# Halved up products, stores and splits on GpSimd, and all ending gathers at once, in a two-layer transformer and mixture-of-experts kernel

## The chip, the cores and the metric

The kernel runs on one core of one Trainium2 chip. The time is the device time of that core in microseconds (us). Before the change it is 2076.37 us, the median of three runs (2075.52 to 2078.95). The engines are TensorE (PE in the profile; PEld is its loading of weights), VectorE (DVE), ScalarE (ACT), GpSimd (POOL) and SyncE (SP). SyncE, ScalarE and GpSimd can issue DMAs.

## The reference

512 tokens of width 1024 go through two transformer layers, then through a third layer whose feed-forward part is a mixture of 16 experts. Only this last part and the ending are touched:

```python
def hier_moe(h, lp):                      # h: 512 tokens x 1024
    g_logits = h @ w_router_group + b_router_group            # 4 groups
    p_group = softmax(g_logits); g_sel = argmax(g_logits)
    e_sel = logits of the 4 experts of that group
    top_v, top_i = top_k(e_sel, 2)
    w_top = softmax(top_v) * p_group[g_sel]
    for e in range(16):
        a = silu(h @ w_gate[e]) * (h @ w_up[e])               # 1024 x 512 each
        y = y + combine[e] * (a @ w_down[e])                  # 512 x 1024
x = x + gate2 * rmsnorm(y, g_post_ffn)
```

All values are float32. Each product is made of three float32r products of a high and a low part of both operands (high x high, low x high, high x low).

## The kernel before

**Routing.** TensorE computes the logits of the router and transposes the normalised tokens; VectorE and ScalarE copy them, and they are stored as `h2_tokens` in HBM. A chain of some 60 small VectorE operations (`seq`), with two exponentials on ScalarE and a few small matmuls, gives each pair of token and expert a slot in a list in which every expert's slots start at a multiple of 128. `seq` waits each time for all that VectorE, ScalarE and TensorE have been given so far. GpSimd scatters the token numbers into the list `slot_token`.

**The expert loop.** A block is 128 slots of one expert. There are 18 blocks in this run; the last one stands behind the loop. A block's weights are 12 units of 128 x 1024: units 0 to 3 are the gate weights, 4 to 7 up, 8 to 11 down. In a block:
- SyncE reads the next block's expert number and fetches that block's 12 units into a ring of 12 buffers (`fetch`, L2201). Each fetch waits until the unit of this block that lies in the buffer has been split.
- ScalarE copies a unit's high part (`split_unit`, L2209), and VectorE subtracts it from the unit, which gives the low part (L2211). Six split units can be held, and they are made four ahead of the products (`split_ahead`).
- TensorE makes 24 gate matmuls and 24 up matmuls (`wide`), each with 512 columns, then waits for the product of silu(gate) and up (`av`, VectorE, L2275), transposes it (4 transposes, L2280), transposes the next block's gathered tokens (8 transposes, `turn_rows`, L2178), waits for the split of the transposed hidden values (ScalarE L2285, VectorE L2287), and makes 24 down matmuls.
- GpSimd gathers the token rows of a later block (`gather`, L2170: 128 rows of 4 KB by an indirect DMA). It does nothing else in the loop. The statement stands in the middle of the block, but GpSimd waits only until the rows gathered last have been transposed, so it runs ahead of the others: as soon as TensorE has transposed the rows for block b + 1, in the middle of block b, the gather for block b + 2 is issued.
- ScalarE and VectorE copy the two halves of the output (L2307, L2310), and SyncE stores it to `slot_output` in HBM (L2313). SyncE waits for the copies first, so it fetches nothing meanwhile.

All queues run in the order in which the code is written; what one engine needs from another it waits for on a semaphore (`reach`).

**The ending.** For each of four groups of 128 tokens GpSimd gathers the two output rows of each token (L2348), two groups at most in flight. VectorE and ScalarE weight and add them, normalise them and add the tokens, which TensorE transposes; ScalarE stores the result.

## Time and profile before

| | |
|---|---|
| Median of three runs | 2076.37 us |
| The profiled execution | 2073.45 us |
| Its span, first to last instruction | 2072.0 us |
| Mean granted TensorE clock | 0.927 |
| TensorE busy | 1820.4 us (88%) |
| VectorE, ScalarE, GpSimd busy | 1227.8, 874.9, 109.5 us |
| Gathers of the expert loop, in number | 18 |
| Stores of a block's output, in number | 18 |

The times in the rows below are microseconds from the start of the span; a matmul's row begins where it begins and has the engine's modelled end, so that the distance between the starts of two matmuls is the pace. "[1.05 <-PE bank L202]" behind a row is the engine's idle time before it and what ended it. A DMA's row is the issuing instruction; when the data has landed is told apart from it. Lines are those of the kernel before.

### The profile page before, as it was taken

How to read it: one execution, taken by the hardware profiler on the slowest of the kernel's cores; microseconds unless marked ns; L12 is line 12 of the kernel's file. 1: busy time of each engine (PE TensorE's matmuls, PEld its weight loads, DVE VectorE, ACT ScalarE, POOL GpSimd, SP SyncE). 2: the span in 40 equal slices, each digit the busy share in tenths (PEclk: the TensorE clock that was granted, in tenths of full speed). 3: DMA queues.
4: the chain of work that ended last, by engine and by line, in shares of the span. 5: the costliest groups of instructions: out<-in, count | busy, mean ns of one | idle time of the engine just before them, and what ended most of it. 6: DMA issues, size and time to landing. Idle time of an engine off the chain costs nothing.

```text
span 2072.0 us, 24514 instructions
## 1 busy us (share of the span) xinstructions
PE 1820.4 (88%) x8710; PEld 1488.0 (72%) x8710; DVE 1227.8 (59%) x2145; ACT 874.9 (42%) x1382; POOL 109.5 (5%) x132
## 2 busy tenths in 40 slices
PE   8897899999998977899999997999687299999982
PEld 7776788888887656788888886866577277777762
DVE  3555668885226555568665226455733388888874
ACT  3346532233215446332323214335622177777761
POOL 1000000000000000001100001000000201001001
PEclk9899899999998989999999997999885599999996
DMA  4323235454331240246543333202110499999963
GB/s 141 94 69 118 62 102 142 133 148 129 100 100 44 71 183 11 71 113 190 163 134 111 102 93 98 82 1 72 51 41 8 166 343 369 361 361 368 359 249 132
DMA packets 224050, 294.57 MB, mean 142 GB/s; under 512 B 13344, under 2 KB 151560, under 8 KB 223832
## 3 DMA queue, kind: packets, MB, share of 16 engines
q1 hardware_dynamic: 205492, 235.36, 34.8%
q0 software_dynamic: 12080, 41.65, 6.4%
q10 hardware_dynamic: 6388, 16.35, 2.1%
q8 instruction: 58, 0.95, 0.2%
q14 instruction: 32, 0.26, 0.0%
HBM read 271.78 MB, written 21.54 MB: 142 GB/s over the span
## 4 chain that ended last, share of the span: by engine, by line
PE 78%; DVE 10%; ACT 7%; issue 2%; DMA 2%; POOL 0%; DVEq 0%; ACTq 0%; POOLq 0%; SPq 0%
PE bank L200 23%; PE bank L202 22%; PE bank L201 22%; PE bank L69 11%; DVE tmp L69 2%; DVE weights_low L227 1%; DMA out_second<-slot_output,pair_slots 1%; ACT weights_high L221 1%; ACT squares L69 1%; DVE z_and_u L69 1%; DVE hidden_low L2287 1%; DVE expert_hidden L2275 1%; PE bank L2280 1%; ACT hidden_high L2285 1%; PE bank L272 0%
## 5 line engine op out<-in xcount | busy, mean ns | idle before, releaser
L227 DVE TENSOR_TENSOR weights_low<-ring,weights_high 128x1024 fp32r<-128x1024 f32 x202 | 246.7, 1223 | 407.4 <-ACT weights_high L221 407.3
L200 PE MATMUL bank<-XH,weights_high 128*128 128x512 f32 x1120 | 454.0, 405 | 30.0 <-DVE XL L69 20.3
L202 PE MATMUL bank<-XH,weights_low 128*128 128x512 f32 x1120 | 444.0, 396 | 0.0
L201 PE MATMUL bank<-XL,weights_high 128*128 128x512 f32 x1120 | 443.3, 396 | 0.0
L221 ACT CAST weights_high<-ring 128x1024 fp32r<-128x1024 f32 x202 | 211.1, 1047 | 439.3 <-PE bank L202 438.2
L200 PEld LDWEIGHTS bank<-XH,weights_high 128*128 128x128 f32 x1120 | 215.4, 192 | 78.7 <-ACT squares L69 12.3
L202 PEld LDWEIGHTS bank<-XH,weights_low 128*128 128x128 f32 x1120 | 214.7, 192 | 47.1
L201 PEld LDWEIGHTS bank<-XL,weights_high 128*128 128x128 f32 x1120 | 215.3, 192 | 42.8 <-issue 0.5
L2211 DVE TENSOR_TENSOR XL<-ring,XH 128x1024 fp32r<-128x1024 f32 x144 | 169.7, 1220 | 31.0 <-ACT XH L2209 31.0
L2209 ACT CAST XH<-ring 128x1024 fp32r<-128x1024 f32 x144 | 143.5, 1046 | 0.0
L69 DVE SCALAR_TENSOR_TENSOR squares<-ring,c_silu,squares 128x128 f32<-128x128 f32 x384 | 135.2, 352 | 13.6
L200 PE MATMUL bank<-hidden_high,weights_high 128*128 128x512 f32 x352 | 137.1, 390 | 0.0
L202 PE MATMUL bank<-hidden_high,weights_low 128*128 128x512 f32 x352 | 137.0, 389 | 0.0
L201 PE MATMUL bank<-hidden_low,weights_high 128*128 128x512 f32 x352 | 136.9, 389 | 0.0
L2211 DVE TENSOR_TENSOR weights_low<-ring,weights_high 128x1024 fp32r<-128x1024 f32 x72 | 86.1, 1218 | 0.1
L189 POOL DMA_DIRECT2D ring<-in_w_ada x48 | 42.5, 885 | 720.0 <-DVE squares L263 720.0
L202 PEld LDWEIGHTS bank<-hidden_high,weights_low 128*128 128x128 f32 x352 | 66.1, 188 | 13.8
L201 PEld LDWEIGHTS bank<-hidden_low,weights_high 128*128 128x128 f32 x352 | 66.1, 188 | 13.8
L200 PEld LDWEIGHTS bank<-hidden_high,weights_high 128*128 128x128 f32 x352 | 66.1, 188 | 13.4
L1111 ACT ACTIVATE tmp<-tmp 128x512 f32<-128x512 f32 x44 | 27.8, 632 | 110.0 <-DVE tmp L1107 110.0
L2209 ACT CAST weights_high<-ring 128x1024 fp32r<-128x1024 f32 x72 | 73.8, 1050 | 0.0
L200 PE MATMUL bank<-XH,hidden_high 128*128 128x512 f32 x144 | 59.9, 416 | 11.7 <-DVE hidden_low L2287 11.7
(445 smaller groups left out, 2953.6 us busy)
## 6 DMA issues: line engine op xcount, KB each, us to landing
ring<-in_w_ffn_in SPq DMA_DIRECT2D x88, 512.0 KB, 4.7
ring<-in_w_gate SPq DMA_DIRECT2D x72, 512.0 KB, 4.9
ring<-in_w_up SPq DMA_DIRECT2D x72, 512.0 KB, 8.5
ring<-in_w_down SPq DMA_DIRECT2D x72, 512.0 KB, 10.5
ring<-in_w_ada POOLq DMA_DIRECT2D x48, 512.0 KB, 4.7
ring<-in_w_ffn_out SPq DMA_DIRECT2D x44, 512.0 KB, 3.5
ring<-in_w_out SPq DMA_DIRECT2D x24, 512.0 KB, 3.5
slot_output<-expert_out SPq DMA_DIRECT2D x18, 512.0 KB, 3.8
```

The costliest lines, as they stand in the source:

```text
L69: op(*args, **kw).then_inc(self.line.sem, 1)
L189: queue.eng.dma_start(dst, src).then_inc(ln.sem, 16)
L200: PE.matmul(out_ap, w_h, x_h, start=first, stop=False, skip_group_check=True)
L201: PE.matmul(out_ap, w_h, x_l, start=False, stop=False, skip_group_check=True)
L202: return PE.matmul(out_ap, w_l, x_h, start=False, stop=last, skip_group_check=True)
L221: S.copy(wh[:, s, :], ring[s][:, :]).then_inc(high_done.sem, 1)
L227: V.tensor_tensor(wl[:, s, :], ring[s][:, :], wh[:, s, :].bitcast(F32), ALU.subtract).then_inc(split_done.sem, 1)
L1111: S.activation(sg, sg, ACT.Silu).then_inc(silu_done.sem, 1)
L2209: S.copy(high[s], raw[q]).then_inc(l_high.sem, 1)
L2211: V.tensor_tensor(low[s], raw[q], high[s].bitcast(F32), ALU.subtract).then_inc(l_split.sem, 1)
L2275: V.tensor_tensor(av[:, :], sg[:, :], bank[1][:, :], ALU.mult).then_inc(l_av.sem, 1)
L2280: t = PE.transpose(bank[6][:, k * P:(k + 1) * P], av[:, k * P:(k + 1) * P], ident)
```

## The change

1. **Up products in halves.** The up matmuls have 256 columns, one half into bank 1 and one into bank 7; there are 48 instead of 24. In unit 7 the first half is finished before the second. `av`, the transposes and the splits of the hidden values are done by halves too; the next block's 8 transposes stand between the two halves' transposes, and the first two down units need only the first half.
2. **Store on GpSimd.** In every block but the last GpSimd issues the store of the output, waits until it has landed, and then tells ScalarE and VectorE that the buffer is free.
3. **Two splits on GpSimd.** The low parts of units 1 and 11 are made by GpSimd.
4. **The gather** for block b + 1 now stands first in block b. On GpSimd's queue that is behind the wait for the store of block b - 1.
5. **Ending.** All 8 gathers are issued at once into buffers of their own; ScalarE does the first weighting and, with the scale and epsilon in it, the root; GpSimd adds the tokens for groups 0 and 1; the gain row is made ahead of the routing chain and the tokens are transposed behind its second exponential (`token_rows`), and `seq` waits only for what it needs.

```diff
+POOLED = (1, 11)
...
-            return vec.do(op, *args, after=[vec.line.now(), act.line.now(), pe.line.now()], **kw)
+            return vec.do(op, *args, after=[vec.line.now(), *after], **kw)
...
+            for c in range(4):
+                k = 4 * half + c
+                t = pe.do(PE.matmul, bank[b][:, c * P:(c + 1) * P], POST_FFN[:, k:k + 1].broadcast_to([P, P]), ident,
+                          start=True, stop=True)
+            bank_free[b] = [act.do(S.copy, grow[:, half * 512:(half + 1) * 512], bank[b][:, :], after=[t])]
...
+                    for c in range(4):
+                        k = 4 * half + c
+                        t = pe.do(PE.transpose, bank[b][:, c * P:(c + 1) * P], X[:, k, t4 * P:(t4 + 1) * P], ident)
+                    bank_free[b] = [act.do(S.copy, x_tok[:, t4, half * 512:(half + 1) * 512], bank[b][:, :], after=[t])]
...
             S.copy(high[s], raw[q]).then_inc(l_high.sem, 1)
-            reach(V, l_high, g + 1)
-            V.tensor_tensor(low[s], raw[q], high[s].bitcast(F32), ALU.subtract).then_inc(l_split.sem, 1)
+            if q in POOLED:
+                reach(G, l_high, g + 1)
+                G.tensor_tensor(low[s], raw[q], high[s].bitcast(F32), ALU.subtract).then_inc(l_pool.sem, 1)
+            else:
+                reach(V, l_high, g + 1)
+                V.tensor_tensor(low[s], raw[q], high[s].bitcast(F32), ALU.subtract).then_inc(l_split.sem, 1)
...
+            if not last:
+                gather(b + 1)
...
+            wait_split(PE, b, 7)
+            up(7, (0,), 0)
+            up(7, (0,), 1).then_inc(l_up.sem, 1)
+            up(7, (1,), 0)
+            up(7, (1,), 1).then_inc(l_used.sem, 1)
+            hidden(0)
+            hidden(1)
+            hidden_turn(0)
+            if not last:
+                turn_rows(b + 1)
+            hidden_turn(1)
             reach(S, l_used, b * UNITS)
+            hidden_split(0)
+            hidden_split(1)
             split_ahead(7)
-            if not last:
-                gather(b + 1)
-                turn_rows(b + 1)
...
-            SP.dma_start(yd[bass.ds(b * P, P), :], yt[:, :]).then_inc(l_st.sem, 16)
+            store = SP if last else G
+            reach(store, l_y0, b + 1)
+            reach(store, l_y1, b + 1)
+            store.dma_start(yd[bass.ds(b * P, P), :], yt[:, :]).then_inc((l_last if last else l_st).sem, 16)
+            if not last:
+                G.wait_ge(l_st.sem, b * 16 + 16)
+                G.sem_inc(l_free.sem, 1)
...
         for t4 in range(TT):
+            for j, dst in enumerate((first, second)):
+                G.indirect_dma_start(dst[:, t4, :], None, yd,
+                                     bass.IndirectOffsetOnAxis(ap=slots_u[:, j, t4:t4 + 1], axis=0)).then_inc(
+                    l_pair[t4].sem, 16)
```

GpSimd in the expert loop, before: from the read of the first table entry to the end of the loop.

```order
L2319 TENSOR_LOAD block_expert
L2321 UNCONDITIONAL_BRANCH
L2321 COMPARE_AND_BRANCH
L2166 REGISTER_ALU
L2167 ISA [waits rows_turned]
L2167 COPY tokens_now<-slot_tokens 128x1
L2168 REGISTER_ALU
L2170 DMA gathered<-h_tokens,tokens_now 128x1024 [waits index_set]
L2321 UNCONDITIONAL_BRANCH
```

GpSimd in the expert loop, after (`XL<-ring,XH` is the split of unit 11, `weights_low<-ring,weights_high` that of unit 1 of the next block, `slot_output<-expert_out` the store).

```order
L2191 ISA [waits rows_turned]
L2191 COPY tokens_now<-slot_tokens 128x1
L2192 REGISTER_ALU
L2194 DMA gathered<-h_tokens,tokens_now 128x1024 [waits index_set]
L2182 ISA
L2243 TENSOR_TENSOR XL<-ring,XH 128x1024 [waits unit_high_done]
L2182 ISA
L2243 TENSOR_TENSOR weights_low<-ring,weights_high 128x1024 [waits unit_high_done]
L2182 REGISTER_ALU
L2388 ISA [waits out1_done,out0_done]
L2388 DMA slot_output<-expert_out 128x1024
L2390 ISA
```

The row that follows in the program is the loop's branch, `L2399 UNCONDITIONAL_BRANCH [waits out_stored]`: GpSimd turns to the next block's gather when the store has landed.

TensorE between the last up product and the first down product, before:

```order
L202 MATMUL bank<-weights_high,gathered_low 128x512
L2158 REGISTER_ALU
L2280 MATMUL bank<-const_tables,expert_hidden 128x128 [waits hidden_low_done,hidden_done]
L2280 MATMUL bank<-const_tables,expert_hidden 128x128 x3
L2175 ISA
L2158 ISA [waits rows_gathered]
L2178 MATMUL bank<-const_tables,gathered 128x128 [waits gathered_low_done]
L2178 MATMUL bank<-const_tables,gathered 128x128 x7
L2158 REGISTER_ALU [waits out1_done,out0_done,hidden_low_done]
L200 MATMUL bank<-XH,hidden_high 128x512 [waits unit_split_done]
```

The same place after:

```order
L203 MATMUL bank<-weights_high,gathered_low 128x256
L2315 MATMUL bank<-const_tables,expert_hidden 128x128 [waits hidden_done]
L2315 MATMUL bank<-const_tables,expert_hidden 128x128
L2199 ISA
L2182 ISA [waits rows_gathered]
L2202 MATMUL bank<-const_tables,gathered 128x128 [waits gathered_low_done]
L2202 MATMUL bank<-const_tables,gathered 128x128 x7
L2315 MATMUL bank<-const_tables,expert_hidden 128x128 [waits hidden_done]
L2315 MATMUL bank<-const_tables,expert_hidden 128x128
L2182 REGISTER_ALU [waits out1_done,out0_done,hidden_low_done]
L201 MATMUL bank<-XH,hidden_high 128x512 [waits unit_split_done]
```

The wait for the gathered rows stands at the same place in the block; the hidden values' transposes are now on both sides of it.

## Rows read from the trace of the kernel before

**Rows 1.** The page, part 4: the chain that ended last, shares of the span by engine

```profile
PE 78%; DVE 10%; ACT 7%; issue 2%; DMA 2%; POOL 0%; DVEq 0%; ACTq 0%; POOLq 0%; SPq 0%
```

**Rows 2.** Chain of waits between up and down products, one block: start us, us, what

```profile
1707.88 0.70 DVE expert_hidden L2275
...
1709.93 0.70 DVE hidden_low L2287
```

**Rows 3.** Timeline, TensorE, one block: start, length, line, operation [idle <-releaser]

```profile
1709.11 1.04 PE L2178 MATMUL bank<-const_tables,gathered 128*128 128x128 f32 x8
...
1710.75 0.50 PE L200 MATMUL bank<-XH,hidden_high 128*128 128x512 f32 x1 [0.60 <-DVE hidden_low L2287]
...
1716.45 0.40 PE L200 MATMUL bank<-weights_high,gathered_high 128*128 128x512 f32 x1
...
1727.42 0.40 PE L202 MATMUL bank<-weights_high,gathered_low 128*128 128x512 f32 x1
```

**Rows 4.** Stretches: length, busy of each engine, granted clock, DMA share, GB/s

```profile
1707.88:1728.04 20.16, 18.60 (x84) 14.71 (x84) 16.99 (x18) 15.48 (x19) 1.85 (x2) 1.00 0.99 359
...
1696.00:1700.00 4.00, 4.00 (x19) 3.22 (x18) 2.72 (x4) 3.46 (x5) 0.00 (x0) 1.00 1.03 411
```

**Rows 5.** The store of a block's output, L2313: one issue; its time to landing

```profile
1718.68 0.35 SPq L2313 DMA_DIRECT2D slot_output<-expert_out  x1
...
DMA to landing us min/median/max: 2.6/3.8/4.2
```

**Rows 6.** The gathers, L2170: two issues, landing of all 18, landing in 1640:1660

```profile
1651.09 0.98 POOL L2170 DMA_INDIRECT gathered<-h_tokens,tokens_now  x1 [0.80 <-POOL tokens_now L2167]
...
1711.28 1.67 POOL L2170 DMA_INDIRECT gathered<-h_tokens,tokens_now  x1 [0.79 <-POOL tokens_now L2167]
...
DMA to landing us min/median/max: 4.4/8.2/8.3
...
gathered<-h_tokens,tokens_now POOLq DMA_INDIRECT x2, 6.3
```

**Rows 7.** The page, part 6: the largest plain DMAs that GpSimd issues

```profile
ring<-in_w_ada POOLq DMA_DIRECT2D x48, 512.0 KB, 4.7
```

**Rows 8.** Waits of SyncE's queue, 1688 to 1990: us in total, times, longest

```profile
SPq L2158 <- DVE expert_out L2310: 88.7, 15, 5.9
```

**Rows 9.** Timeline, TensorE, where 512 and 256 columns meet

```profile
1347.48 0.39 PE L202 MATMUL bank<-XH,weights_low 128*128 128x512 f32 x1
...
1347.70 0.28 PE L200 MATMUL bank<-ctx_high,weights_high 128*128 128x256 f32 x1
...
1347.82 0.28 PE L201 MATMUL bank<-ctx_low,weights_high 128*128 128x256 f32 x1
```

**Rows 10.** The last block: TensorE's timeline, then a stretch with the granted clock

```profile
2013.05 0.66 PE L2280 MATMUL bank<-const_tables,expert_hidden 128*128 128x128 f32 x4 [1.55 <-DVE expert_hidden L2275]
...
2015.19 0.79 PE L200 MATMUL bank<-XH,hidden_high 128*128 128x512 f32 x1 [1.48 <-DVE hidden_low L2287]
...
2020.47 0.61 PE L200 MATMUL bank<-XH,hidden_high 128*128 128x512 f32 x1
...
2014.00:2015.00 1.00, 0.00 (x0) 0.00 (x0) 0.64 (x1) 1.00 (x2) 0.00 (x0) 0.55 0.00 0
```

**Rows 11.** Groups by form in one block: mean ns of VectorE's part and ScalarE's

```profile
L2211 DVE TENSOR_TENSOR XL<-ring,XH 128x1024 fp32r<-128x1024 f32 x8 | 9.4, 1220 | 1.5 <-ACT XH L2209 1.5
...
L2209 ACT CAST XH<-ring 128x1024 fp32r<-128x1024 f32 x8 | 8.0, 1047 | 0.0
```

**Rows 12.** The ending: a gather's issue, and pieces of the chain of waits

```profile
2030.04 0.94 POOL L2348 DMA_INDIRECT out_second<-slot_output,pair_slots  x1 [0.30 <-issue]
...
2030.04 5.12 DMA out_second<-slot_output,pair_slots
...
2062.72 0.77 DVE out_first L69
```

**Rows 13.** Timeline, ScalarE, in the routing

```profile
1604.53 1.28 ACT L69 ACT_TABLE_LOAD   x1 [1.00 <-DVE r_logits L69]
```

More of the change, by code:

```diff
@@ new lines, in up, with hidden @@
+            def up(q, halves, c):
+                s, k = q % HELD, 2 * (q - 4) + c
+                for n in halves:
+                    cols = slice(c * DE + n * 256, c * DE + (n + 1) * 256)
+                    t = three_pass(bank[(1, 7)[n]][:, 0:256], hgh[:, k, :], hgl[:, k, :], high[s][:, cols],
+                                   low[s][:, cols], k == 0, k == KC - 1)
+                return t
+            def hidden(n):
+                if n == 0:
+                    reach(V, l_up, b + 1)
+                    reach(V, l_silu, b + 1)
+                    reach(V, l_at, b * 2)
+                else:
+                    reach(V, l_used, b * UNITS + 8)
+                V.tensor_tensor(av[:, n * 256:(n + 1) * 256], sg[:, n * 256:(n + 1) * 256], bank[(1, 7)[n]][:, 0:256],
+                                ALU.mult).then_inc(l_av.sem, 1)
@@ L2257, in block, with down @@
+            def down(q):
+                s, k = q % HELD, q - 8
+                wait_split(PE, b, q)
+                for n in range(2):
+                    t = three_pass(bank[2 + n][:, :], ath[:, k, :], atl[:, k, :], high[s][:, n * 512:(n + 1) * 512],
+                                   low[s][:, n * 512:(n + 1) * 512], k == 0, k == 3)
+                t.then_inc(l_used.sem, 1)
+            if not last:
+                gather(b + 1)
             reach(S, l_table, b)
@@ new lines, in program @@
+        first, second = sbuf("out_first", [P, TT, D]), sbuf("out_second", [P, TT, D])
+        ss, root = sbuf("sum_squares", [P, TT]), sbuf("out_root", [P, TT])
+        l_pair, lout = [line(f"pair_gathered{t4}") for t4 in range(TT)], line("output_stored")
+        root_table()
+        for t4 in range(TT):
+            for j, dst in enumerate((first, second)):
+                G.indirect_dma_start(dst[:, t4, :], None, yd,
+                                     bass.IndirectOffsetOnAxis(ap=slots_u[:, j, t4:t4 + 1], axis=0)).then_inc(
+                    l_pair[t4].sem, 16)
+                l_pair[t4].n += 16
@@ new lines, in program, with pair_sum @@
+        summed, scaled = {}, {}
+        def pair_sum(t4):
+            t = act.do(S.activation, first[:, t4, :], first[:, t4, :], ACT.Copy, scale=wts[:, 0, t4:t4 + 1],
+                       after=[l_pair[t4].now()])
+            vec.need(l_pair[t4].now())
+            summed[t4] = vec.do(V.scalar_tensor_tensor, first[:, t4, :], second[:, t4, :], wts[:, 1, t4:t4 + 1],
+                                first[:, t4, :], ALU.mult, ALU.add, after=[t])
+            t = act.do(S.activation, second[:, t4, :], first[:, t4, :], ACT.Square, accum_out=ss[:, t4:t4 + 1],
+                       after=[summed[t4]])
+            t = act.do(S.activation, root[:, t4:t4 + 1], ss[:, t4:t4 + 1], ACT.Sqrt, scale=1.0 / D,
+                       bias=epsilon[:, 0:1], after=[t])
+            return t
@@ new lines, in finish_tokens @@
+        def finish_tokens(t4, rooted):
+            t = vec.do(V.reciprocal, root[:, t4:t4 + 1], root[:, t4:t4 + 1], after=[rooted])
+            scaled[t4] = vec.do(V.scalar_tensor_tensor, first[:, t4, :], first[:, t4, :], root[:, t4:t4 + 1], grow[:, :],
+                                ALU.mult, ALU.mult, after=[t])
+            q = pool if t4 < 2 else vec
+            t = q.do(q.eng.tensor_tensor, first[:, t4, :], first[:, t4, :], x_tok[:, t4, :], ALU.add, after=[scaled[t4]])
+            load((sp, act)[t4 % 2], lout, out[0, t4 * P:(t4 + 1) * P, :], first[:, t4, :], after=[t])
@@ L2371, in program @@
+        rooted = pair_sum(0)
+        for t4 in range(1, TT):
+            following = pair_sum(t4)
+            finish_tokens(t4 - 1, rooted)
+            rooted = following
+        finish_tokens(TT - 1, rooted)
         for q in (act, sp):
-            q.need(lout[0].now(), lout[1].now())
+            q.need(lout.now())
 INPUTS = [
```

151 lines of the change are left out of this document (64 added, 87 removed).

## The prediction, made before the changed kernel ran

> **What bounds the kernel now.** I read the page's chain first: 78% of the span is TensorE [rows 1]. Then I took the expert loop by itself, since four of the five parts of the change lie there or behind it. A block lasts 20.16 us, at full clock and with the DMA engines busy at 0.99 [rows 4]. I laid one block out from the timeline of TensorE [rows 3]. The gate products begin at 1716.45; I call such a moment D, since the down products have just ended. The last up product begins at 1727.42, so 48 matmuls of 512 columns take 11.2 us, 0.233 each. Down runs from 1710.75 to 1716.45: 5.70 us. What is left, 3.2 us, is the way from up to down: the product on VectorE, 0.70, four transposes, the cast on ScalarE, and the subtraction on VectorE, 0.70 [rows 2]; the next rows' 8 transposes, 1.04, lie in it [rows 3]. No weight unit is waited for. The DMA engines are nearly full, but a block moves 14 transfers of 512 KB (12 units, a gather, a store), 7.34 MB, and at the 411 GB/s of a full stretch [rows 4] that is 17.9 us, below every block time that follows. So TensorE and its handoffs bound the loop, and GpSimd is idle in it for most of the time: that freedom is what hides the gather today. It is issued at 1711.28, right behind the transposes that free its buffer [rows 3, 6], and its rows are wanted a whole block later.
>
> **Up in halves.** The matmuls of 256 columns follow each other after 0.12 us, those of 512 after 0.22 [rows 9], so the 24 pairs cost about 24 x 0.0125 = 0.3 us per block. In exchange the product, the transposes and the split of the first half run beside other work. A block without any wait would be: gate and up 11.2 + 0.3; the first half's transposes, reached 0.35 after that; the next rows 1.04; the second half's transposes and handoff 0.2; down 5.70. Sum 18.8 us, 1.36 less than now.
>
> **Store on GpSimd, and what stands behind it.** Taking the store off SyncE ends SyncE's wait of 5.9 us per block [rows 8]. That is worth nothing by itself, since no engine waits for weights; it keeps the DMA engines evenly loaded. But GpSimd's queue is now: gather, split of unit 11, split of unit 1, store, wait for the store's landing, next gather. The gather that was issued a block ahead is issued only when the store before it has landed, and its rows are wanted within the same block, at D + 11.9 (11.5 plus 0.35). I follow that chain from D:
> - store issued: 2.23 us after D, as now (1718.68 less 1716.45) [rows 3, 5];
> - store landed: SyncE's own landed after 3.8 us [rows 5], in the lull that SyncE's parking makes; that is the lower end. The upper end is a loaded gather's 8.2 [rows 6]. The nearest row is a plain DMA of the same size that GpSimd issues, 4.7 us [rows 7]; I take that;
> - gather issued: 1.13 us later (1711.28 less the transposes' end at 1710.15) [rows 3, 6];
> - gather landed: 4.4 to 8.3 us, with 8.2 the median of 18 [rows 6]. The short one is the very first. The second, issued at 1651.09 among the fetches, already took 8.2 (the two have a median of 6.3 [rows 6]). In the new kernel it is issued amid the fetches for units 4 to 10, so I take 8.2, and 4.4 as the lower end.
>
> Sum: 2.23 + 4.7 + 1.13 + 8.2 = 16.3 us, against 11.9: TensorE waits 4.4 us. Behind the wait stand, in TensorE's queue, the rows' transposes, the second half's transposes and down, 1.04 + 0.2 + 5.70 = 6.9 us, with the handoffs some 7.2. Block: 16.3 + 7.2 = 23.5 us, 3.3 more than now. It is a loop: down's end, store, gather, down's end; nothing in it runs ahead. With both ends low it is 11.6, no wait; with both high 19.9.
>
> **The clock.** In the last block TensorE is idle for 1.55 and then 1.48 us, with 0.66 us of transposes between. The granted clock in 2014 to 2015 is 0.55, that is 1.2 GHz for most of it. The twelve matmuls from 2015.19 to 2020.47 are 0.44 us apart [rows 10], against 0.24 in other blocks' down [rows 3]: 12 x 0.2 = 2.4 us lost. A wait of 4.4 us is longer than both gaps together, so I expect the same in each waiting block, with 0.6 for transposes at that clock: 3.0 us. Block 26.5, 6.3 more than now.
>
> **Two splits on GpSimd.** VectorE has 2 of 12 subtractions of 1.22 us less [rows 11]; it does not bound the block, so that saves nothing. No row shows such a subtraction on GpSimd. It can hardly be shorter than VectorE's 1.22; above no row bounds it, but its slack does: unit 11's cast (1.05 us on ScalarE [rows 11], behind the second half's, about 0.4) ends some 4.2 us before D, and unit 1 is wanted a quarter of the gate products, 1.4, after D, so two of up to 2.8 us fit. I take nothing for it; at three times VectorE's, 3.7 us, a block pays 2 x 0.9 = 1.8, the other end. The Trainium skill has a price for it (GPSIMD Engine Reference, Elementwise — side-by-side cycle accounting): 4497 ns for 2048 elements, by which an estimate for 1024 is 2.25 us, and the sum would be the same.
>
> GpSimd's gather instruction lasts 0.98 us where VectorE is between splits and 1.67 where it is in one [rows 6]. The Trainium skill (SBUF — State Buffer, SBUF: two separate sides) says that GpSimd and VectorE instructions with two SBUF inputs shut each other out for their whole length; the 0.7 agrees. By that rule the two subtractions would hold VectorE's splits up as well, which speaks against the change and is the third rival below.
>
> **Ending.** Now, a second gather of a pair lands 5.12 us after its issue at 2030.04, so the first pair is there at 2035.2; the last pair is there at 2062.7, and 9.3 us follow [rows 12]. A gather alone took 4.4 us [rows 6]; the second of the pair landed 1.25 + 5.12 = 6.4 after the first one's issue (one issue is 0.94 + 0.30 us), so a further gather adds 2.0. With all 8 issued at once the pairs then land 4 us apart, the last at 2047.2, 15 us earlier. At the pace of issue, 2.5 us a pair, it would be 20; without any overlap of transfers, 0. I take 15. The work per pair, two VectorE passes of 1.3 us, fits beside the next landing.
>
> **Routing.** The gain row's two ScalarE copies stand ahead of the first exponential and its table load of 1.28 us, which now runs early [rows 13]: up to 2 us later, I take 1.5. The shorter waits in `seq` save nothing, as the operations follow each other on one engine.
>
> **Sum.** 16 blocks wait (block 0's gather precedes any store, the last block has none): 16 x 6.3 = 101. The other two gain 1.4 each: -3. Ending -15, routing +1.5. Against the profiled execution of 2073.45: 2158. The median of the runs is 2.9 above that execution; I leave it out.
>
> **Rivals.**
> - *The gather is there in time* (faster). For it: with SyncE never parked the transfers are spread evenly, and 3.8 + 4.4 us have both been seen [rows 5, 6]. It decides below 8.5 us for the two together. Against it: at 18.8 us a block the DMA engines would have 17.9 us of work, hence no quiet stretch for either. Time: 2073.45 - 18 x 1.36 - 15 + 1.5 = 2035; 2048 where small waits remain. Chance 0.20.
> - *The wait is there, the clock stays.* 16 x 3.3 = 53, so 2110; with the store at 3.8 us 2096. For it: a block still has some 19 us of dense work around the wait. Chance 0.26.
> - *GpSimd's splits come too late.* No gather wait, but 1.8 us for units 11 and 1: 2035 + 17 x 1.8 = 2066. Against it: slack as above. Chance 0.05.
> - *Forecast:* wait and clock, 2125 to 2190 with the store between 3.8 and 6.5 us. Chance 0.49.
>
> A measurement of this kernel tells 0.2%, 4 us, from no change. Faster takes the first rival and half of the third, 0.22; within 0.2% 0.03; slower 0.75. The range, 2048 to 2192, leaves out the fastest cases and a store of 8 us in each block.
>
> **What would show it.** TensorE's first rows' transpose idle for 4 to 5 us before it, released by the gather's DMA, in 16 blocks; the gather's issue about 8 us after D and GpSimd waiting for the store's landing before it; a block of 26 to 27 us; the granted clock at 0.5 after each wait. If the blocks last under 20 us, or the rows' transposes wait for nothing, the forecast is wrong at the landings; if the wait is there and the clock is 1.00, at the clock. The ending is right if the last pair lands some 19 us after the last store.

## The result and the profile after

The changed kernel takes 2208.4 us (median of four runs, 2206.39 to 2212.03), the kernel before on the same chip 2075.94 (2072.37 to 2078.95): a ratio of 1.064 [1.0617, 1.0664], slower by 133 us. The forecast was 2158 with a range of 2048 to 2192. It has the sign and the mechanism, and it misses the size by 50 us.

I read the page of the changed kernel's profile first (span 2210.5 us, clock 0.899, before 0.927): busy time, then the shares of the chain that ended last.

```profile
PE 1852.5 (84%) x9142; PEld 1536.8 (70%) x9142; DVE 1223.3 (55%) x2129; ACT 888.0 (40%) x1415; POOL 216.7 (10%) x187
...
PE 66%; DMA 12%; DVE 9%; ACT 7%; issue 5%; POOL 1%; POOLq 0%; DVEq 0%; ACTq 0%; SPq 0%
```

TensorE has fallen from 78% of the chain [rows 1] to 66%, and DMA has come in with 12%, before 2%. Next the waits between 1700 and 2090 us (who waited for whom: us in total, times, the longest):

```profile
PE bank L2202 <- DMA gathered<-h_tokens,tokens_now: 111.7, 14, 8.4
POOL tokens_now L2191 <- DMA slot_output<-expert_out: 89.4, 13, 7.2
PE bank L201 <- DVE gathered_low L2211: 1.5, 4, 0.5
```

TensorE waits 8.0 us in each of the 14 blocks in this window for the gathered rows, and GpSimd 6.9 us for the store before it issues the gather. The timeline of GpSimd for one block and the start of the next (start, length, line, operation, idle before):

```profile
1737.78 3.38 POOL L2243 TENSOR_TENSOR weights_low<-ring,weights_high 128x1024 fp32r<-128x1024 f32 x1
1744.74 0.58 POOL L2388 DMA_DIRECT2D slot_output<-expert_out  x1 [3.58 <-DVE expert_out L2384]
1752.51 0.18 POOL L2191 COPY tokens_now<-slot_tokens 128x1 uint32 x1 [7.20 <-DMA slot_output<-expert_out]
1753.49 1.00 POOL L2194 DMA_INDIRECT gathered<-h_tokens,tokens_now  x1 [0.80 <-POOL tokens_now L2191]
1764.96 2.40 POOL L2243 TENSOR_TENSOR XL<-ring,XH 128x1024 fp32r<-128x1024 f32 x1 [10.47 <-ACT XH L2240]
1767.33 3.37 POOL L2243 TENSOR_TENSOR weights_low<-ring,weights_high 128x1024 fp32r<-128x1024 f32 x1
1774.28 0.58 POOL L2388 DMA_DIRECT2D slot_output<-expert_out  x1 [3.57 <-DVE expert_out L2384]
```

And TensorE's timeline in the same block, which answers to [rows 3]: the first row is D, the end of the last down product; then the transposes of the first half, of the next rows, the first down product, a later one, and the next D.

```profile
1740.33 0.49 PE L201 MATMUL bank<-weights_high,gathered_high 128*128 128x512 f32 x1
...
1752.31 0.44 PE L2315 MATMUL bank<-const_tables,expert_hidden 128*128 128x128 f32 x2 [0.53 <-DVE expert_hidden L2308]
1761.13 1.97 PE L2202 MATMUL bank<-const_tables,gathered 128*128 128x128 f32 x8 [8.38 <-DMA gathered<-h_tokens,tokens_now]
...
1763.75 0.63 PE L202 MATMUL bank<-XL,hidden_high 128*128 128x512 f32 x1
1764.18 0.63 PE L203 MATMUL bank<-XH,hidden_low 128*128 128x512 f32 x1
...
1770.30 0.39 PE L201 MATMUL bank<-weights_high,gathered_high 128*128 128x512 f32 x1
```

The chain of the forecast can be read off: D at 1740.33, store issued 4.4 later (4.0 in the next block), gather issued 8.75 after that (7.1 to the landing, the rest handoff), transposes 7.64 after that, next D another 9.17 later. Over all 16 such blocks the distance between two stores is (2153.94 - 1686.00) / 16 = 29.25 us, against 20.15 before. 16 x 9.1 is 146 us, more than the whole loss.

From trace to trace the difference of the spans, 2210.5 less 2072.0 = 138.5 us, closes from its pieces. The first store is issued 7.6 us later than before (1686.00, 1678.40), the 16 blocks between stores take 145.6 more, the last block, from store to store, 4.5 less (19.80, before 24.27), and the stretch from the last store's issue to the end 10.2 less.

Stretches of two microseconds of this block (length, busy of each engine, granted clock, DMA share, GB/s), which answer to [rows 4, 10]:

```profile
1754.00:1756.00 2.00, 0.00 (x0) 0.00 (x0) 0.00 (x0) 0.00 (x0) 0.49 (x1) 1.00 1.06 400
1758.00:1760.00 2.00, 0.00 (x0) 0.00 (x0) 0.00 (x0) 0.00 (x0) 0.00 (x0) 0.50 1.02 406
1762.00:1764.00 2.00, 2.00 (x10) 1.90 (x9) 0.03 (x1) 0.44 (x2) 0.00 (x0) 0.50 0.00 0
1766.00:1768.00 2.00, 2.00 (x10) 1.58 (x9) 2.00 (x1) 2.00 (x4) 2.00 (x2) 0.92 0.00 0
```

The granted clock falls to 0.50 (1.2 GHz) while TensorE waits, and is still 0.50 in the stretch from 1764; in the stretch from 1766 it is 0.92, with TensorE at work since 1761.13. In the wait the DMA engines run full (400 GB/s) with the fetches and the gather; from 1762 to 1768, with the rows landed and no fetch under way, they stand still.

### The profile page after: what moved, and what is told of

It is laid out like the page before. It is cut to its first block, busy times and chain, and to the rows that moved or that the text cites. A ratio compares the mean times of both kernels' runs of the same rounds, so it can differ in the third digit from the quotient of the medians.

```text
span 2210.5 us, 25500 instructions
## 1 busy us (share of the span) xinstructions
PE 1852.5 (84%) x9142; PEld 1536.8 (70%) x9142; DVE 1223.3 (55%) x2129; ACT 888.0 (40%) x1415; POOL 216.7 (10%) x187
## 4 chain that ended last, share of the span: by engine, by line
PE 66%; DMA 12%; DVE 9%; ACT 7%; issue 5%; POOL 1%; POOLq 0%; DVEq 0%; ACTq 0%; SPq 0%
PE bank L201 18%; PE bank L203 18%; PE bank L202 18%; PE bank L70 10%; DMA gathered<-h_tokens,tokens_now 6%; DMA slot_output<-expert_out 5%; DVE tmp L70 2%; PE bank L2202 2%; DVE weights_low L228 1%; DVE XL L2246 1%; ACT weights_high L222 1%; ACT squares L70 1%; DVE z_and_u L70 1%; DVE out_first L70 1%; DVE expert_out L2384 0%
## 5 line engine op out<-in xcount | busy, mean ns | idle before, releaser
L222 ACT CAST weights_high<-ring 128x1024 fp32r<-128x1024 f32 x202 | 211.3, 1048 | 444.3 <-PE bank L203 443.4
L2202 PE MATMUL bank<-const_tables,gathered 128*128 128x128 f32 x144 | 34.4, 419 | 159.1 <-DMA gathered<-h_tokens,tokens_now 159.1
L2202 PEld LDWEIGHTS bank<-const_tables,gathered 128*128 128x128 f32 x144 | 27.5, 219 | 162.9 <-issue 131.6
L2325 DVE TENSOR_TENSOR hidden_low<-bank,hidden_high 128x256 fp32r<-128x256 f32 x36 | 15.2, 425 | 170.7 <-ACT hidden_high L2323 170.7
L2323 ACT CAST hidden_high<-bank 128x256 fp32r<-128x256 f32 x36 | 13.4, 372 | 213.1 <-PE bank L2315 213.1
L201 PE MATMUL bank<-weights_high,gathered_high 128*128 128x256 f32 (+1 forms) x216 | 70.5, 327 | 7.4 <-DVE weights_low L2246 3.4
```

What stands on the lines that cost most here:

```text
L201: PE.matmul(out_ap, w_h, x_h, start=first, stop=False, skip_group_check=True)
L222: S.copy(wh[:, s, :], ring[s][:, :]).then_inc(high_done.sem, 1)
L2202: t = PE.transpose(bank[4 + k // 4][:, (k % 4) * P:(k % 4 + 1) * P], hg[:, k * P:(k + 1) * P], ident)
L2323: S.copy(ath[:, dst, :], src).then_inc(l_ath.sem, 1)
L2325: V.tensor_tensor(atl[:, dst, :], src, ath[:, dst, :].bitcast(F32), ALU.subtract).then_inc(l_atl.sem, 1)
```

## The experiments

Each ran on one chip beside the kernel before, and ratios are to those runs; code is cut to what matters. A block's length is the mean distance of two stores over 16 blocks. "Changed kernel" is the kernel after the change.

**1. GpSimd waits for the store only after the next gather.** Moved: the wait for the landing, and the freeing of the output buffer, to behind `gather(b + 1)` of the next block.

```diff
-            if not last:
-                G.wait_ge(l_st.sem, b * 16 + 16)
-                G.sem_inc(l_free.sem, 1)
 # next block
             if not last:
                 gather(b + 1)
+            G.wait_ge(l_st.sem, b * 16 + 16)
+            G.sem_inc(l_free.sem, 1)
```

> The changed kernel, but GpSimd waits for the store's landing only after it has issued the next gather (a 4-byte DMA ahead of the loop makes the counts start at one). Theory (the chain down's end, store, store's landing, gather, gather's landing sets the block): 7.1 us of landing leave the chain. The gather is issued at about D + 6.1 and has landed at D + 13.6, and TensorE is there at D + 11.9 to 13.0: a wait of 0.6 to 1.7 us is left. A block lasts 20.8 to 22.2 us instead of 29.3; 16 blocks: 2072 to 2094 us. Rival A (GpSimd's subtractions and their hold on VectorE are most of the loss): they stay, so no more than 20 us less, 2188 or more. Rival B (transfers that GpSimd issues are slow, whatever waits for them): the gather's landing stays the end of a wait as long as now, 2170 or more.

Measured: 2102.3 us, ratio 1.013 [1.0106, 1.0153]; block 22.41. So 106 us hang on that one wait. The time is 8 us above the expected range. The gather is now issued 2.5 us after the store (1728.77 and 1731.30), and a wait of 2.0 us for its rows is left in each block, against the expected 0.6 to 1.7. Rivals A and B fall: GpSimd's subtractions are all still there, and so are GpSimd's DMAs.

**2. The gather ahead of the store.** `gather(b + 1)` at the block's start becomes `gather(b + 2)` behind unit 11's subtraction; the wait behind the store stays. One gather of rows that nobody uses is left over at the end (19 instead of 18).

```diff
-            if not last:
-                gather(b + 1)
...
             split_ahead(7)
+            if not last:
+                gather(b + 2)
```

> The changed kernel, but a block gathers the rows of block b + 2 right behind the transposes that free the buffer, ahead of GpSimd's second subtraction and of the store; the wait behind the store stays. Theory (the gather queued behind the store's landing is the loss): the whole chain is gone, TensorE does not wait for rows and the granted clock stays at 1.00 there; block 19 to 20.5 us, time 2025 to 2060 us, below the kernel before. Rival A (GpSimd's subtractions are most of it): 2150 or more, since both remain and the gather now stands ahead of one. Rival B (the queue of GpSimd's own transfers is slow): the store's landing of 7 us now ends no wait but the next subtraction's; unit 11's split comes late, and the block keeps 23 us or more: 2100 and above.

Measured: 2077.7 us, ratio 1.0018 [1.0005, 1.0031]; block 21.10. The chain is gone: no row for the gathered rows is left in TensorE's waits. But the time is 18 us above the expected range, and the waits between 1700 and 2000 us name where:

```profile
PEld bank L201 <- POOL weights_low L2243: 29.4, 15, 2.0
PE bank L201 <- POOL weights_low L2243: 22.8, 15, 1.5
```

Unit 1's subtraction stands on GpSimd behind the gather (issued at 1738.97, subtraction from 1739.99) and comes 1.5 us late in each block. Here what the forecast called its third rival is real, in another place.

**3. No subtraction on GpSimd.** `POOLED = (1, 11)` becomes `POOLED = ()`.

> The changed kernel with all twelve subtractions on VectorE; store on GpSimd as changed. Theory (chain, with GpSimd's subtractions delaying the output copy by about 2 us): the store is issued at D + 2.2 instead of D + 4.4, and the rest of the chain stays: 16 x 2.2 = 35 us less, about 2173 us. Rival A (the subtractions are most of the loss): 2100 or less. Rival C (the late copy comes from TensorE's clock or the copies themselves, not from GpSimd): no change, 2200 or more.

Measured: 2183.5 us, ratio 1.051 [1.0482, 1.0537]; block 27.60. 25 us less, of the 35 expected. The store is issued at D + 3.3 (1740.16, D at 1736.82): 1.1 earlier, not 2.2. Its row and those of VectorE ahead of it:

```profile
1730.90 0.42 DVE L2325 TENSOR_TENSOR hidden_low<-bank,hidden_high 128x256 fp32r<-128x256 f32 x1 [8.80 <-ACT hidden_high L2323]
...
1736.46 2.35 DVE L2246 TENSOR_TENSOR XL<-ring,XH 128x1024 fp32r<-128x1024 f32 x2
1738.73 0.68 DVE L2384 COPY expert_out<-bank 128x512 f32<-128x512 f32 x1
1740.16 0.57 POOL L2388 DMA_DIRECT2D slot_output<-expert_out  x1 [18.90 <-DVE expert_out L2384]
```

In the changed kernel the same two subtractions last 3.37 instead of 2.35, because GpSimd subtracts at the same time:

```profile
1740.02 3.37 DVE L2246 TENSOR_TENSOR XL<-ring,XH 128x1024 fp32r<-128x1024 f32 x2
1743.30 0.68 DVE L2384 COPY expert_out<-bank 128x512 f32<-128x512 f32 x1
```

In the kernel before the copy has the same place in VectorE's queue, behind the same two subtractions:

```profile
1709.93 0.69 DVE L2287 TENSOR_TENSOR hidden_low<-bank,hidden_high 128x512 fp32r<-128x512 f32 x1 [1.37 <-ACT hidden_high L2285]
...
1717.76 0.68 DVE L2310 COPY expert_out<-bank 128x512 f32<-128x512 f32 x1
```

So of the 2.2 us by which the store's issue was forecast too early, 1.1 in this block is GpSimd's hold on VectorE (the copy ends at D + 3.65, without GpSimd's subtractions at D + 2.59). The other half is there without it. VectorE needs 8.51 us from the start of `hidden_low` to the end of the copy in both kernels (1709.93 to 1718.44, 1730.90 to 1739.41), but D now comes 5.9 us after that start and not 6.5: 0.6. Down now begins on the first half of the hidden values. And from the copy's end to the store's issue SyncE took 0.24 us (1718.68) and GpSimd takes 0.75: 0.5.

**4. TensorE filled with work while it waits.** 28 matmuls of 512 columns into bank 0 ahead of the next rows' transposes.

```diff
             hidden_turn(0)
             if not last:
+                for _ in range(28):
+                    PE.matmul(bank[0][:, :], hgh[:, 0, :], hgh[:, 0:4, :].rearrange("p k n -> p (k n)"), start=True,
                              stop=True, skip_group_check=True)
                 turn_rows(b + 1)
```

> The changed kernel with 28 matmuls of 512 columns into a free bank in front of the next rows' transposes (28 x 0.22 = 6.2 us of the 7.6 us wait). Their results are not used. Theory of the clock: it stays at 1.00 through the wait, and the transposes and the first down products are as quick as in the kernel before: 3 us less per block, 16 x 3 = 48, about 2160 us. Rival D (the clock comes back by itself in time, or what is slower lies beside another wait): 2200 or more; if the fillers themselves run at half clock they end after the gather has landed and the time rises above 2230.

Measured: 2200.3 us, ratio 1.0594 [1.0566, 1.0621]; block 28.08. By its time this run lies where rival D stood. The clock does stay at 1.00, as the stretch before the transposes shows (its columns as above), and the eight transposes take their 1.09 us.

```profile
1766.00:1768.00 2.00, 0.60 (x4) 0.18 (x3) 0.00 (x0) 0.00 (x0) 0.00 (x0) 1.00 0.81 324
```

The timeline of TensorE has the start of the gate products and, in the next block, the transposes:

```profile
1747.69 0.49 PE L201 MATMUL bank<-weights_high,gathered_high 128*128 128x512 f32 x1 [0.76 <-DVE gathered_low L2211]
...
1767.90 1.09 PE L2202 MATMUL bank<-const_tables,gathered 128*128 128x128 f32 x8 [1.40 <-DMA gathered<-h_tokens,tokens_now]
```

But a block gains only 1.2 us. At half clock the transposes cost 0.9 more and seven down matmuls 0.2 more each, 2.3 us together; at full clock TensorE reaches the gate products before the rows' low part is ready and waits 0.76 (first row); to that extent what was slower did lie beside another wait. The fill costs some 8 us once, in the first block, whose rows come without a wait: its store is at 1695.14 instead of 1686.00, of which 1.3 was there before the first gather. So the clock's price was expected at 3.0 per block, and it is 1.2: the wait alone is nearly all of the loss.

**5. The gather ahead, and no subtraction on GpSimd.** Experiments 2 and 3 together.

> The run in which the next gather but one stands ahead of the store, and all twelve subtractions on VectorE. With GpSimd's subtractions a block of that run lasts 21.10 us, TensorE waiting 1.5 us for unit 1's. Theory (the two subtractions cost time of their own, since GpSimd and VectorE shut each other out): block 18.8 to 19.3 us, time 2040 to 2050 us. Rival (the DMA engines, with 7.34 MB a block, are the bound as soon as nothing else is): block 20 us or more, 2058 or above. Rival (the late unit is only a matter of its place behind the gather): no change, 2075.

Measured: 2046.9 us, ratio 0.9873 [0.9846, 0.9899]; block 19.27, steady to 0.02. The store is still on GpSimd, which still waits for it (5.5 us landing, median), and the kernel is faster than before: neither the store's place nor its wait costs anything that experiment 7 (2047.4 us, block 19.27) would show, where no gather stands behind the wait.

**6. The store back on SyncE**, the subtractions left on GpSimd.

```diff
-            store = SP if last else G
-            reach(store, l_y0, b + 1)
-            reach(store, l_y1, b + 1)
-            store.dma_start(...)
-            if not last:
-                G.wait_ge(l_st.sem, b * 16 + 16)
-                G.sem_inc(l_free.sem, 1)
+            reach(SP, l_y0, b + 1)
+            reach(SP, l_y1, b + 1)
+            SP.dma_start(yd[bass.ds(b * P, P), :], yt[:, :]).then_inc(l_st.sem, 16)
```

> The changed kernel with the store issued by SyncE as before the change; the two subtractions stay on GpSimd. Theory (queue order on GpSimd): the gather stands behind unit 1's subtraction only, is issued at about D + 2.6 and lands before it is wanted; what is left are the subtractions, block 20.5 to 21.2 us, 2065 to 2085 us. Rival (a gather that is issued in the block in which it is used is late in any case): TensorE waits for rows, 2100 or more.

Measured: 2055.8 us, ratio 0.9917 [0.9888, 0.9945]; block 19.86. The gather is issued at 1759.17 with D at 1756.43 (D + 2.7) and is in time. The block is 0.6 us and the time 9 us below the expected range: the subtractions cost less here than in experiment 2, where one of them stood behind the gather.

**7. Halves and new ends alone.** Experiment 6 with `POOLED = ()`.

> Of the change only the up products in halves, the new ending and the new routing; stores on SyncE, all subtractions on VectorE. Theory: the halves save 1.2 to 1.4 us of the 20.16 us of a block, ending -10 us, routing +3 us: 2044 to 2050 us. Rival (nearly full DMA engines take the gain back, or SyncE parked behind the store does): block 20.0 us or more, 2062 or above.

Measured: 2047.4 us, ratio 0.9867 [0.9842, 0.9892]; block 19.27. With experiment 6 this prices the two subtractions on GpSimd where no chain hangs on them: 0.59 us per block, 8.4 us in all. In experiment 6 TensorE waits 0.5 us in each block for `expert_hidden` from VectorE, and in experiment 7 it does not. With experiment 5 it says that SyncE or GpSimd as the store's issuer makes no difference.

**8. Only the new routing and ending**, with the loop of before.

> The kernel before with only the new routing and the new ending. From the two traces: the ending 10 us shorter, the routing 3 to 7 us longer, the loop as it was: 2068 to 2073 us. By the prediction's own terms (ending -15, routing +1.5): 2062.

Measured: 2062.0 us, ratio 0.9936 [0.9916, 0.9955], 12.4 us less than before. My expectation from the two traces was at least 6 us too high. The time agrees with the prediction's own two terms, by which it was 2062, but by chance: in the traces the first store comes 1.1 us later than before, the ending takes 10.2 less and not 15, and the last block, which the edit does not touch, takes 2.6 less (21.66 us from store to store, before 24.27). 2.4 of that last piece are the clock's: the twelve matmuls of [rows 10], 0.44 us apart there, are 0.23 apart here. TensorE waits as long there as in [rows 10], 1.54 and 1.47 us, and the granted clock stays at 1.00:

```profile
2015.00:2016.00 1.00, 0.00 (x0) 0.00 (x0) 0.53 (x1) 1.00 (x2) 0.00 (x0) 1.00 0.00 0
```

With experiment 7, the halves are worth 14.6 us, 0.88 per block.

**9. The store's and the gather's company.** The store lands in 6.8 us (median) in the changed kernel, against 3.8 before. Four kernels ask why. In two of them SyncE holds back the next block's units, 4 to 11 or all twelve, until the store has landed; in a third it holds back units 8 to 11 until the gathered rows are transposed; in the fourth SyncE issues the store, and GpSimd waits for it as in the changed kernel. The expectations stand in the order 4 to 11, 8 to 11, all twelve, SyncE's store.

```diff
                 for q in range(UNITS):
+                    if q == 4:      # 0 in the second, 8 in the third
+                        reach(SP, l_gate, b * (UNITS - len(POOLED)) + 4)   # ... + 1, ... + 8
                     fetch(b + 1, e, q)
...
                 G.sem_inc(l_free.sem, 1)
+                G.sem_inc(l_gate.sem, 10)   # the store has landed; in the third TensorE does it, behind the rows' transposes
```

```diff
 # the fourth: experiment 6, and behind the store
+            if not last:
+                reach(G, l_st, b * 16 + 16)
```

> The changed kernel, but SyncE fetches the next block's units 4 to 11 only after the store before has landed. Theory (the store took 7.1 us and not the 4.7 us of the forecast because it shares the DMA engines with the fetches): it lands in 2.7 to 4.7 us, 2.4 to 4.4 us leave each of 16 blocks, 2138 to 2170 us. Rival (a store that GpSimd issues takes 7 us by itself): no change, 2200 us or more.

> The changed kernel, but SyncE fetches the next block's units 8 to 11 only after the gathered rows have been transposed. Theory (the gather's 7.5 us are a share of loaded DMA engines): it lands in 4.4 to 5.0 us, 2.5 to 3.1 us leave each of 16 blocks, 2158 to 2168 us. Rival (the loaded landing does not come from these fetches, or the later fetches come too late for the next block): no change or slower, 2200 us or more.

> The changed kernel, but SyncE fetches nothing for the block after next until the store has landed, the four gate units included. Theory (company of fetches makes the store slow, and the four gate fetches that were left alone in the run before are company enough): the store lands in 2.7 to 4.0 us instead of 6.8. The gather then has all twelve fetches beside it, 8.2 to 9.5 us: the block loses 1.5 to 3 us, 2160 to 2190 us. Rival (GpSimd's stores are slow by themselves): landing 6 us, and the time rises to 2220 or more.

> The changed kernel, but SyncE issues the store, in its old place behind the fetches, and GpSimd still waits for its landing before it issues the next gather. Theory (company of fetches): SyncE is parked for the copies and issues no gate fetch ahead of the store, so it lands in 3 to 4.5 us; 2.5 to 3.5 us leave each block, 2150 to 2170 us. Rival (landing is long whoever issues and whatever else runs): 2195 or more. Theory of the chain: in any case far above the 2056 us of the same kernel without GpSimd's wait.

| | time, us (ratio) | block | store landed, median | gather landed, median |
|---|---|---|---|---|
| changed kernel | 2208.4 (1.0641) | 29.25 | 6.8 | 7.5 |
| units 4 to 11 held for the store | 2223.0 (1.0718) | 30.1 | 6.1 | 8.6 |
| all units held for the store | 2183.8 (1.0521) | 27.6 | 2.9 | 7.8 |
| units 8 to 11 held for the gather | 2161.8 (1.0416) | 26.2 | 6.8 | 4.4 |
| SyncE stores, GpSimd waits | 2159.3 (1.0400) | 26.2 | 2.6 | 8.4 |

The first run missed: I had overlooked that the four gate units, fetched just ahead of the store, are enough company. In the changed kernel SyncE issues them right before GpSimd's store at 1744.74:

```profile
1739.57 4.35 SPq L2232 DMA_DIRECT2D ring<-in_w_gate  x4
```

The first run gained 0.7 us on the store, lost 1.1 on the gather, and came out slower. The other three decide it. A DMA of 512 KB landed in 2.6 to 2.9 us (store) or 4.4 us (gather) where the fetches had been taken from beside it, and in 6.1 to 8.6 us beside fetches. With all units held GpSimd issued the store, and it took 2.9, so the issuer is not the cause:

```profile
1767.31 0.58 POOL L2392 DMA_DIRECT2D slot_output<-expert_out  x1 [3.57 <-DVE expert_out L2388]
1771.01 0.31 POOL L2193 COPY tokens_now<-slot_tokens 128x1 uint32 x1 [3.12 <-DMA slot_output<-expert_out]
```

The fourth is also the second proof of the chain. Experiment 6 and it differ in one wait of GpSimd, 2055.8 against 2159.3 us: 6.3 us per block. And SyncE's being parked for the copies, which the change set out to end, is what lets the store land quickly in the waiting loop. In the loops without the chain it is worth little: the median landing is 5.0 us in experiment 7, with SyncE parked, and 5.5 in experiment 5, with the store on GpSimd.

**10. The first forecast of the block without waits.** In experiments 5 and 7 a block takes 19.27 us and not 18.8. The gate products wait for the rows' low part:

```profile
1774.36 0.50 PE L201 MATMUL bank<-weights_high,gathered_high 128*128 128x512 f32 x1 [0.54 <-DVE gathered_low L2211]
```

The last edit of the study makes both halves of the rows' split ahead of unit 1's (on top of experiment 11).

```diff
-                if q < 10 and not last:
-                    split_rows(b + 1, q - 8)
+                if q == 8 and not last:
+                    split_rows(b + 1, 0)
+                    split_rows(b + 1, 1)
```

> The run with the ending without GpSimd (2044.3 us), with both halves of the next rows' split made ahead of unit 1's, so that the gate products do not wait 0.55 us for the rows' low part at their start. Theory: 0.5 us less in each of 17 blocks, 2035 to 2037 us. Rival (unit 1's and the following splits come later by the same time, and VectorE, busy 90%, is the bound): 2042 or more.

Measured: 2040.7 us, ratio 0.9820 [0.9807, 0.9834]; block 19.04. It is the fastest kernel here. It gained 0.23 per block where 0.5 was expected, between the two theories. The wait for the rows' low part is gone, and TensorE waits 0.56 us for `expert_hidden` from VectorE later in the block instead.

**11. The ending and the routing.** On top of experiment 7: VectorE makes all four additions and SyncE issues all output stores; then, on top of that, the gain row's matmuls and copies stand behind the second exponential.

```diff
-            q = pool if t4 < 2 else vec
+            q = vec
...
-            load((sp, act)[t4 % 2], lout, ...)
+            load(sp, lout, ...)
```

> The run with halves, stores on SyncE and all subtractions on VectorE (2047.4 us), but in the ending VectorE adds the tokens for all four groups and SyncE issues all output stores. Theory (the ending is bound by the ScalarE and VectorE work per group, and GpSimd's two additions slow VectorE and hold up ScalarE's queue by 2.7 us): 2 to 5 us less, 2042 to 2045 us. Rival (the last pair's landing bounds it): no change.

Measured: 2044.3 us, ratio 0.9855 [0.9832, 0.9877], 3.1 less than experiment 7; the two intervals overlap, but the rows show the cause. In experiment 7 the addition on GpSimd lies beside a VectorE pass, which takes 2.25 instead of 1.28, and ScalarE, whose queue stores the second group, stands 2.74 us until the other addition is done:

```profile
2028.12 2.34 POOL L70 TENSOR_TENSOR out_first<-out_first,x_tokens 128x1024 f32<-128x1024 f32 x1 [4.61 <-DVE out_first L70]
2029.29 2.25 DVE L70 SCALAR_TENSOR_TENSOR out_first<-out_second,pair_weights,out_first 128x1024 f32<-128x1024 f32 x1 [1.26 <-ACT out_first L70]
2035.79 1.15 ACT L70 ACTIVATE out_first<-out_first,pair_weights 128x1024 f32<-128x1024 f32 x1 [2.74 <-POOL out_first L70]
```

> As the run with the ending without GpSimd, and the gain row's eight matmuls and two copies moved behind the second exponential. Theory (they stand ahead of the first exponential's table load on the way to the first gather): 1 to 3 us less than that run. Rival (the tokens' transposes and copies, which stand on ScalarE as well, take their place): within 1 us of it.

Measured: 2049.2 us, ratio 0.9874 [0.9854, 0.9895]: not faster, if anything slower. The first exponential's table load does come sooner behind the logits' copy, but eight more matmuls and two copies then stand among the work on the way to the counts. From the logits' copy to the first scatter of the routing it is 29.1 us in its trace, against 23.9 without the edit. Of the 2.8 us that the changed kernel's routing takes longer than before, the rows place 1.4 at the first exponential: from the start of `r_exp` to that of `r_product` it is 1.2 us before and 2.6 after (1605.4 to 1606.6, 1610.2 to 1612.8). No run here settles the rest.

## Why the prediction was wrong

The mechanism held at every step that was named: the wait is at the first row transpose, released by the gather, in 16 blocks; GpSimd waits for the store before it; the clock is at 0.5 after it. The sizes did not: the idle time is 8.0 us and not 4 to 5, and the gather is issued 13.2 us after D and not 8. One line of the forecast, the sum of the loop, carried the error. Term by term for one block, the measured column from the block shown above:

| term | forecast | measured | settled by |
|---|---|---|---|
| D to store issued | 2.23 | 4.4 | experiment 3: 1.1 from GpSimd's hold on VectorE, 0.6 from an earlier D, 0.5 from GpSimd's slower issue |
| store issued to landed | 4.7 | 7.1 | experiment 9: fetches beside it |
| handoff to the gather | 1.13 | 1.66 | rows of GpSimd |
| gather issued to transposes | 8.2 | 7.64 | experiment 9 |
| transposes to the next D, with the clock | 7.2 + 3.0 | 9.17 | experiment 4 |
| sum | 26.5 | 30.0 | mean of 16 blocks: 29.25 |

- **The step that failed is "I take that" for the store's landing.** The forecast put the landing between 3.8 and 8.2 us, and took 4.7 because a plain DMA of GpSimd stood in the page [rows 7]. Those are DMAs of another stage, with other company. The same paragraph took a loaded 8.2 for the gather, issued 6 us later into the same stream of fetches. The store deserved the same reasoning: with SyncE no longer parked, the fetches for the gate units are issued right ahead of it. The cost was 2.4 us a block, 38 us.
- **"2.23 us after D, as now" was the second.** It kept the old distance from D to the store, although the same change lets down end sooner against VectorE's queue, puts a competitor on VectorE's way and gives the store to an engine that issues it later. That cost 2.2 us a block, 35 us. The forecast quoted the Trainium skill (SBUF — State Buffer, SBUF: two separate sides), by which GpSimd and VectorE instructions with two SBUF inputs shut each other out for their whole length, and kept it for a rival; it should have stood in this term. The rows bear the rule out: the subtraction that begins first takes 2.40 us on GpSimd and 1.22 on VectorE, the one that meets the other 3.37 and up to 2.60.
- **The clock was sized too high**, 3.0 against 1.2 (experiment 4). The twelve slow matmuls of the last block [rows 10] were carried over as they stood; after these waits seven were slow, and part of what they lose lies beside VectorE's split of the rows. Nor is the drop in [rows 10] a steady one: with the same idle times it is missing in experiment 8. Without the clock's 1.2 the last term would be 8.0, where 7.2 was forecast.
- **The block without waits** was put at 18.8 and is 19.27 (experiment 7), of which 0.54 to 0.57 is the wait at the end of down for the rows' low part (experiment 10).
- **The subtractions on GpSimd**, forecast at nothing within 0 to 1.8, cost 0.59 per block without the chain. Their length was right: 2.40 where nothing holds them, as the slack allowed for. What they cost is time on VectorE's side: 0.5 of the 0.59 is TensorE's wait for `expert_hidden`.
- **The ending** gave 10 us instead of 15: last store landed to the end 44.2 before, 34.1 after. The forecast bounded it by landings 4 us apart. The gathers came at the pace of issue: the last pair is there some 16 us after the last store's landing, sooner than the 19 that was to show the term right. So landings are not the bound; what bounds it is the work per group, 3.9 us on ScalarE and VectorE (the weighting passes start at 2021.69, 2025.63, 2029.57 and 2033.51 in experiment 11), with 3.1 lost to GpSimd's part.
- **The routing**: 1.5 forecast. The first gather is issued 7.6 us later than before, of which 4.8 are there already when the logits begin, in stages that the change does not touch; 2.8 is the routing's (experiment 11).

The corrected sum: forecast 2158; 16 x (29.25 - 26.5) = +44; ending +5, routing +1; 2208. That it meets the median to a microsecond is partly luck. Two things are left out of it: the 4.8 us ahead of the logits, and the two blocks that do not wait, forecast at 1.4 less each. In the traces the first gains nothing (34.9 us from the first gather to the first store in both), and the last gains 4.5, part of which is the clock's [rows 10]. The rival "the wait is there, the clock stays" (2110) is refuted by the clock rows, though its thought was partly right: the clock cost little. "The gather is there in time" is what experiments 5 to 7 made true by another order, and its 2048, where small waits remain, is near what experiments 5 and 7 measured (2046.9 and 2047.4); with an ending 5 us short and a block 0.5 us longer than forecast, that is partly chance. Experiment 6, with the subtractions on GpSimd, took 2055.8.

Of the five parts, then: halves -0.88 us per block, store on GpSimd 0 by itself, two subtractions +0.59 per block, ending and routing together -12.4 us (2.4 of them the last block's clock, in the traces); and +9.4 us per block (29.25 less 19.86) from something that is no part at all but the order of GpSimd's queue: a gather behind a store's landing. The halves and the new ending survive in the fastest version, experiment 10's.

## What to carry to other kernels

When work is moved to an idle engine, write down that engine's whole queue first: what used to run ahead because the engine was free may now stand behind a wait, and what it hid becomes a chain. A landing time is read from a row with the same company, not from one with the same issuer; where the change removes a pause in the other traffic, the quick landing of before goes with it. And a delay that is read between two engines, here from TensorE's last product to the store behind VectorE's copy, does not carry over when either side moves: count it on the queue that makes it.

## What the runs showed of the hardware

- A store of 512 KB landed in 2.6 to 2.9 us with the fetches held away from it and in 6.8 beside them; a gather of the same size in 4.4 and 7.5 to 8.6 (experiment 9). One of each in a row makes 7 or 15 us.
- GpSimd's subtraction of 128x1024 (float32 inputs from SBUF) took 2.40 us where it began first and 3.37 where VectorE's held it up; VectorE's took 1.22 by itself and up to 2.60 where GpSimd's had begun. Two out of twelve moved to GpSimd left VectorE no less busy: 1223.3 us, and 1224.6 with none moved (experiment 3).
- Matmuls without use kept the granted clock at 1.00 through a wait of 8 us, and a block was 1.2 us shorter for it, not the 2.3 us that the slow instructions had lost (experiment 4).
- After waits of 1.5 and 1.5 us on TensorE in the last block the granted clock was 0.50 in the kernel before and 1.00 in experiment 8, and the block differed by 2.6 us.
